# Values of latent attention for two pairs at once, store by tiles, and feature sums in two rounded parts

## The reference

```python
def rms_norm(x, w):
    xf = x.astype(jnp.float32)
    y = xf * lax.rsqrt(jnp.mean(xf * xf, axis=-1, keepdims=True) + NORM_EPS)
    return (y * w.astype(jnp.float32)).astype(x.dtype)
...
    q = (rms_norm(cq, q_lora_norm) @ w_uq).reshape(bsz, seqlen, H, MLA_NOPE + MLA_ROPE)
    kv = (rms_norm(ckv, kv_lora_norm) @ w_ukv).reshape(bsz, seqlen, H, MLA_NOPE + MLA_V)
    k_nope, v = jnp.split(kv, [MLA_NOPE], axis=-1)
...
    q_nope = rms_norm(q_nope, q_nope_norm)
    q_rope = apply_rope(rms_norm(q_rope, q_rope_norm), cos[:, None, :], sin[:, None, :])
    k_nope = rms_norm(k_nope, k_nope_norm)
...
        p = jax.nn.softmax(jnp.where(mask, s, -jnp.inf), axis=-1).astype(v.dtype)
        return jnp.einsum('bhqk,bkhv->bqhv', p, v)
```

## Time and profile before

| | us |
|---|---|
| median of 3 runs | 2898.31 |
| the profiled execution | 2898.93 |
| its span in the trace | 2897.1 |
| TensorE matmul busy | 2864.6 (99%) |
| TensorE weight load busy | 2326.3 (80%) |
| GpSimd busy | 1848.9 (64%) |
| VectorE busy | 1301.5 (45%) |
| ScalarE busy | 565.8 (20%) |

### The profile page before, as it was taken

One profiled execution on the slowest core, in us unless ns is written; L12 is line 12 of the kernel. 1 busy time (PEld: TensorE's weight loads), 2 busy tenths in 40 slices (PEclk: granted clock), 3 DMA queues, 4 the chain that ended last, 5 costly groups with the idle time before them and its releaser, 6 DMA issues.

```text
span 2897.1 us, 36332 instructions
## 1 busy us (share of the span) xinstructions
PE 2864.6 (99%) x13536; PEld 2326.3 (80%) x13536; DVE 1301.5 (45%) x1506; ACT 565.8 (20%) x821; POOL 1848.9 (64%) x1822
## 2 busy tenths in 40 slices
PE   9999999999989999999999999999999999999998
PEld 6778888888867778888888888788888777788887
DVE  5765545414355654414444223444244455543241
ACT  4550221000124541000111101210001445300000
POOL 5557548777752238777775565677777544677775
PEclk9999999999999999999999999999999999999999
DMA  4112213232220102222232222222322111222322
GB/s 152 61 60 88 74 57 111 80 108 100 84 85 28 38 29 87 92 103 102 80 125 85 74 94 81 73 100 80 105 95 91 69 63 54 72 95 84 106 92 89
DMA packets 38583, 242.35 MB, mean 84 GB/s; under 512 B 4288, under 2 KB 4672, under 8 KB 16608
## 3 DMA queue, kind: packets, MB, share of 16 engines
...
## 4 chain that ended last, share of the span: by engine, by line
PE 94%; DVE 3%; ACT 1%; DVEq 1%; issue 0%; ACTq 0%; DMA 0%; SPq 0%
PE ps L402 67%; PE ps L435 13%; PE ps L1345 1%; PE ps L1161 1%; PE ps L1301 1%; PE ps L1180 1%; PE ps L1382 1%; PE ps L1362 1%; PE ps L1395 1%; PE ps L1377 1%; PE ps L1291 1%; DVEq L2262 0%; DVEq L1857 0%; PE ps L1053 0%; DVE scr L2235 0%
## 5 line engine op out<-in xcount | busy, mean ns | idle before, releaser
L716 POOL CAST w_hi<-raw 128x512 fp32r<-128x512 f32 (+1 forms) x909 | 677.5, 761 | 1030.7 <-PE ps L402 836.7
L704 POOL TENSOR_TENSOR w_lo<-raw,w_hi 128x512 fp32r<-128x512 f32 (+1 forms) x909 | 1220.0, 1354 | 0.1
L402 PE MATMUL ps<-h_hi,w_hi 128*128 128x512 f32 x1904 | 751.7, 395 | 3.3 <-DVE h_lo L1868 3.0
L402 PE MATMUL ps<-h_hi,w_lo 128*128 128x512 f32 x1904 | 742.0, 390 | 0.0
L402 PE MATMUL ps<-h_lo,w_hi 128*128 128x512 f32 x1904 | 741.5, 389 | 0.0
L402 PEld LDWEIGHTS ps<-h_hi,w_hi 128*128 128x128 f32 x1904 | 357.8, 188 | 80.8 <-issue 5.3
L402 PEld LDWEIGHTS ps<-h_hi,w_lo 128*128 128x128 f32 x1904 | 357.6, 188 | 75.7
L402 PEld LDWEIGHTS ps<-h_lo,w_hi 128*128 128x128 f32 x1904 | 357.9, 188 | 75.1 <-issue 2.9
L402 PE MATMUL ps<-a_hi,w_hi 128*128 128x512 f32 x816 | 319.7, 392 | 2.2 <-issue 1.4
L402 PE MATMUL ps<-a_hi,w_lo 128*128 128x512 f32 x816 | 318.3, 390 | 0.0
L402 PE MATMUL ps<-a_lo,w_hi 128*128 128x512 f32 x816 | 318.1, 390 | 0.0
...
## 6 DMA issues: line engine op xcount, KB each, us to landing
...
raw<-weights SPq DMA_DIRECT2D x8, 512.0 KB, 3.5
x<-x_in SPq DMA_DIRECT2D x8, 256.0 KB, 6.3
x_out<-x SPq DMA_DIRECT2D x1, 2048.0 KB, 6.3
...
```

Source lines behind the costliest of these rows:

```text
L402: mm = pe.matmul(out_ap, a, b, start=(i == 0 and not begun), stop=(i == n - 1 and ended))
L704: pool.tensor_tensor(w_lo[:, slot, parts[j]], raw[:, slot, parts[j]], w_hi[:, slot, parts[j]].bitcast(F32), ALU.subtract).then_inc(s_split ...
L716: pool.tensor_copy(w_hi[:, slot, piece], raw[:, slot, piece]).then_inc(s_hi[j], 1)
```

## The change

Five parts:

1. The norms' sum of squares and retention's are split by VectorE into a rounded part and a remainder, and ones are copied rounded. TensorE takes two float32r matmuls where it took a float32 one.
2. In gated linear attention tile 0 of block 1 goes ahead of the last mean.
3. The values of two pairs are projected together. Chunks of even pairs hold 1536 columns (queries, keys, values of two pairs), those of odd pairs 1024. `proj_v` runs in pairs 1, 3 and 5, in two parts of 12 matmuls of 256 columns, and for pairs 0 and 1 ahead of the loop.
4. Queries are handled by heads: mean, root, scaling and rotation of head 0, then of head 1. Mean 0 goes ahead of the turned scores of head 0, keys ahead of the turned scores of head 1. At the head of the stage, VectorE's five constant copies go to ScalarE, as does the rotary part of k for the second buffer, and the two latents for keys and values come between the queries' remainders.
5. Each tile of `x` is stored as soon as it is final.

```diff
+                k, v = (i["w_ukv"][0].reshape(256, 16, 2, 64)[:, :, part].reshape(256, 1024) for part in range(2))
+                kv = [k[:, 128 * u:128 * u + 128]] + ([v[:, 128 * u:128 * u + 256]] if u % 2 == 0 else [])
+                kv = cols_of(*kv)
+                out.append(np.concatenate([q, block(kv, slice(0, 256), slice(0, kv.shape[1]))], axis=1))
...
-STAGE_WIDTHS = {"ssd": [384] + [2048] * 15, "gla": [2048] * 15, "mla": [2048] * 3 + [1280] * 8 + [2048] * 4,
+STAGE_WIDTHS = {"ssd": [384] + [2048] * 15, "gla": [2048] * 15, "mla": [2048] * 3 + [1536, 1024] * 4 + [2048] * 4,
...
         norm_sq = scr[:, scratch_len - 8 * T:scratch_len].rearrange("p (k t) -> p k t", k=8)
+
+        n_hi, n_lo, n_ones = a_hi[:, 6, :], a_lo[:, 6, :], a_hi[:, 5, 0:P]
...
-            sp.wait_ge(s_res, 8 * n_res + 2)
-            sp.dma_start(out, x[:, :, :]).then_inc(s_out, 16)
-            sp.wait_ge(s_out, 16)
+            for k in range(KD):
+                sp.wait_ge(s_res, 8 * (n_res - 1) + k + 3)
+                sp.dma_start(out[:, k, :], x[:, k, :]).then_inc(s_out, 16)
+            sp.wait_ge(s_out, 16 * KD)
...
             def norm(name):
                 pe.wait_ge(s_acc, norm_of[name])
-                pe.matmul(ps[:, norm_bank(name), :], ones, norm_sq[:, 0, :], start=True, stop=True).then_inc(s_mean, 1)
+                pe.matmul(ps[:, norm_bank(name), :], n_ones, n_hi, start=True, stop=False)
+                pe.matmul(ps[:, norm_bank(name), :], n_ones, n_lo, start=False, stop=True).then_inc(s_mean, 1)
...
+                residual_begun("gla", (0,), 1)
                 mean(hd)
-                residual_begun("gla", range(6), 1)
+                residual_begun("gla", range(1, 6), 1)
...
+
+                def proj_v(w, part):
+                    if part == 0:
+                        pe.wait_ge(s_mln, 2 * w + 2)
+                    else:
+                        pe.wait_ge(s_mr, 3 * w + 3)
+                    for tb in (2 * part, 2 * part + 1):
                         s = slice(tb * P, (tb + 1) * P)
-                        mm = product(pe, ps[:, 7, s], [(h_hi[:, k, s], h_lo[:, k, s], *kv_weights(par, k, P))
-                                                       for k in range(2)])
-                    mm.then_inc(s_used, 1)
-
-                def q_means(w):
-                    for e in range(2):
-                        pe.wait_ge(s_msl, 2 * w + e + 1)
-                        pe.matmul(ps[:, 6 + e, :], m_blkq, m_sqh[:, e, :], start=True, stop=False)
...
+                    pe.matmul(ps[:, 6 + e, :], m_blkq, m_sqh[:, e, :], start=True, stop=False)
+                    pe.matmul(ps[:, 6 + e, :], m_blkq, m_sql[:, e, :], start=False, stop=True).then_inc(s_mm, 1)
 
                 def k_mean(w):
...
 
-                    pe.wait_ge(s_mv, u + 1)
...
+                    if ahead:
+                        q_mean(u + 1, 0)
+                    else:
                         residual_begun("mla", (2,))
                     scores_turned(u, par, 0)
                     if ahead:
-                        q_means(u + 1)
+                        q_mean(u + 1, 1)
+                        proj_k(u + 1, nxt)
                     else:
                         residual_begun("mla", (3,))
                     scores_turned(u, par, 1)
                     if ahead:
-                        proj_k(u + 1, nxt)
-                        proj_v(u + 1, nxt)
+                        if par:
+                            proj_v(u + 1, 0)
                         k_mean(u + 1)
                     weighted(u, par, 0)
+                    if ahead and par:
+                        proj_v(u + 1, 1)
...
-                q_means(0)
+                pe.wait_ge(s_mcr, 3)
+                q_mean(0, 0)
+                q_mean(0, 1)
                 pe.wait_ge(s_mh, 5)
                 proj_k(0, 0)
                 k_mean(0)
                 proj_v(0, 0)
+                proj_v(0, 1)
+                pe.wait_ge(s_mkrope, 2)
                 pair(0, 0, True, True)
                 with pe.Fori(0, 3) as i:
...
                     pe.wait_ge(s_radd, hd + 1)
-                    pe.matmul(ps[:, 4, :], ones, r_sq[:, 0, :], start=True, stop=True).then_inc(s_rsum, 1)
+                    pe.matmul(ps[:, 4, :], r_ones, r_sqh, start=True, stop=False)
+                    pe.matmul(ps[:, 4, :], r_ones, r_sql, start=False, stop=True).then_inc(s_rsum, 1)
...
-                def q_squared(w, first=False):
+                act.activation(m_ident, phase_const("mla", "mla_ident"), ACT.Copy)
+                act.activation(m_mask, phase_const("mla", "mla_mask"), ACT.Copy)
+                act.activation(m_blkq, const("blkq"), ACT.Copy)
...
+                def q_rstd(w, e):
+                    act.wait_ge(s_mm, 3 * w + e + 1)
+                    act.activation(m_r[:, e, :], ps[:, 6 + e, :], ACT.Ln, bias=EPS).then_inc(s_mln, 1)
+                    settled().activation(m_r[:, e, :], m_r[:, e, :], ACT.Exp, scale=-0.5).then_inc(s_mr, 1)
...
+                def v_copied(w, n, slot, part):
+                    if slot == 0 and part:
+                        wait_used(c0 + 3 + w)
+                    elif slot == 0:
+                        act.wait_ge(s_mvp, n + 1)
+                    ins = act.activation(
+                        m_v[:, slot, 2 * part:2 * part + 2, :].rearrange("p t (x n) -> p t x n", x=3)[:, :, 0:3:2, :],
+                        ps[:, 7 - part, :].rearrange("p (t w e n) -> p t w e n", t=2, w=2, e=2)[:, :, slot, :, :], ACT.Copy)
+                    if part:
+                        ins.then_inc(s_mv, 1)
 
...
-                def pair(u, par, first, ahead):
+                def pair(u, par, ahead, n):
                     if ahead:
                         q_squared(u + 1)
+                        q_rstd(u + 1, 0)
                     exps(u, 0)
                     if ahead:
-                        q_rstd(u + 1)
+                        q_rstd(u + 1, 1)
+                        k_squared(u + 1, not par, n)
                     exps(u, 1)
                     if ahead:
-                        k_squared(u + 1)
-                        v_copied(u + 1, 1 - par, first)
                         k_rstd(u + 1)
+                    if ahead and par:
+                        v_copied(u + 1, n, 0, 0)
                     sums_inverted(u, 0)
+                    if ahead and par:
+                        v_copied(u + 1, n, 0, 1)
                     sums_inverted(u, 1)
-
+                    if ahead and par:
+                        for part in range(2):
+                            v_copied(u + 2, n, 1, part)
+
+                q_squared(0, True, (0,))
...
+                q_rstd(0, 1)
+                k_squared(0, False, 0)
                 k_rstd(0)
-                v_copied(0, 0, True)
-                pair(0, 0, True, True)
+                act.wait_ge(s_mkrope, 1)
+                act.activation(m_k[64:112, 1, :, :], m_k[64:112, 0, :, :], ACT.Copy).then_inc(s_mkrope, 1)
+                for slot in range(2):
+                    for part in range(2):
...
                 dve.wait_ge(s_sq, 8 * n + k + 1)
-                ins = settled().tensor_tensor(norm_sq[:, 0, :], norm_sq[:, 0, :], norm_sq[:, k, :], ALU.add)
+                settled().tensor_tensor(norm_sq[:, 0, :], norm_sq[:, 0, :], norm_sq[:, k, :], ALU.add)
                 if k == KD - 1:
-                    ins.then_inc(s_acc, 1)
+                    dve.tensor_copy(n_ones, ones)
...
-                    rope_in_k(w)
+                                      ALU.add).then_inc(s_mkrope, 1)
+
...
-                def q_normed(w):
+                def q_ready(w, par, e):
                     dve.drain()
-                    dve.wait_ge(s_mr, 2 * w + 1)
-                    dve.scalar_tensor_tensor(m_raw[:, 0:2, :], m_raw[:, 0:2, :], m_qgain, m_r[:, 0:2, :],
-                                             ALU.mult, ALU.mult)
+                    dve.wait_ge(s_mr, 3 * w + e + 1)
+                    dve.scalar_tensor_tensor(m_raw[:, e, :], m_raw[:, e, :], m_qgain, m_r[:, e, :], ALU.mult, ALU.mult)
                     dve.drain()
-                    turned_products(m_t, m_raw[:, 0:2, :], True)
-
-                def q_ready(par):
-                    dve.tensor_tensor(m_q[:, par, :, :], m_raw[:, 0:2, :], over_heads(cos), ALU.mult)
-                    settled().tensor_tensor(m_q[64:112, par, :, :], m_q[64:112, par, :, :], m_t[64:112, :, :], ALU.add)
+                    turned_products(m_t[:, e, :], m_raw[:, e, :])
...
-                    dve.tensor_scalar(h_hi[:, 6 + e, :], cos, 0.0, None, ALU.mult)
                 q_square_low(0, 0)
                 dve.wait_ge(s_mcr, 3)
+                latent_normed(3)
                 q_square_low(0, 1)
-                for k in (3, 4):
-                    latent_normed(k)
-                q_normed(0)
-                q_ready(0)
+                latent_normed(4)
+                q_ready(0, 0, 0)
...
```

(4 more changed lines are left out.)

87 lines of the change are left out of this document (41 added, 46 removed).

## The result

The changed kernel takes 2878.76 us, the median of 4 runs (2877.41 to 2880.24), against 2898.43 for the kernel before, run beside it: a ratio of 0.993, with a 95% interval of 0.9915 to 0.9946. It is faster by 19.7 us, 0.7%. I had forecast 2874 with a range of 2867 to 2881. The profiled execution took 2880.04 us with a span of 2878.2, 18.9 us under the span of before; my sum had said 24.2.

The account below looks back on a forecast made before the run. The prediction took TensorE as the bound, near a tie in latent attention's pairs with the chain TensorE, ScalarE, VectorE. Terms 4.4 + 1.4 + 4.4 + 10.7 + 3.3 = 24.2 us off 2898.93 gave 2874.7, median 0.6 lower: 2874; range 2867 to 2881.

Parts of the forecast that it names:

- Gain 0.40 x 11, all on the path: Norms and retention means: two products of rounded parts save 0.40 us at each of 11 sums, 4.4 us in all.
- I take no cost: Norms and retention: VectorE's three added operations, at most 3.5 us, fit in 3.7 to 3.9 us of room.
- Weights are never waited for: Whole kernel: no row of TensorE's waits names GpSimd or a DMA.
- I kept 11.2 us: Head of latent attention: the 11.2 us from the start of k's product to the first scores stay unchanged.
- the clock stays up: Rival, head of latent attention: shorter idle pieces keep the clock up; gain 28 us, 2870 us; chance 0.12.
- The forecasts of 23.6 and 25.7: Latent attention: pairs without values last 23.6 us, released by VectorE's k gains; pairs with values last 25.7.
- pairs 0, 2, 4, 6 gain 2.4 each: Latent attention: the pairs without values shrink to 23.6 us, a gain of 2.4 us each.
- pair 7 has no successor and stays: Latent attention: the last pair keeps its time, with no gain or loss.
- The full stop: Rival, shared port: VectorE loses 3.7 us per pair without values, which lasts 24.9; 2879 us; chance 0.17.
- The cold pair: Rival, latent attention: long idle time drops the clock, up to 20 us more per pair; 2966 us; chance 0.01.
- my point of 3.65: Latent attention: pairs turn cold if VectorE's chain ends over 3.65 us behind TensorE.
- The store that does not shrink: Rival, final store: the tail is a fixed cost or stores queue; gain 20.9 us, 2877 us; chance 0.12.

Follow-up runs that it names:

- second profile of the changed kernel: The changed kernel with nothing altered, run again with more runs: 2878.93 us, median of 5; its profile has a span of 2877.1 us.
- 2.9 alone: The kernel before with only the sums in two rounded parts (7 norms, 4 retention means): 2895.46 us in 10 runs, ratio 0.9987.
- 1.37 undone: The changed kernel with gated linear attention's tile 0 of block 1 put back behind the last mean: 2882.38 us, one run.
- 6.3 alone: The kernel before with only latent attention's changes, head and pairs together: 2885.96 us in 5 runs, ratio 0.9958.
- 4.25 alone: The kernel before with only the store of x by tiles: 2894.28 us in 10 runs, ratio 0.9988.
- run with casts: The changed kernel with each of GpSimd's two casts of a chunk without values made five times in pairs 0, 2 and 4: 2879.38 us, 4 runs.
- doubled run: The changed kernel with GpSimd subtracting twice for low parts of chunks without values in pairs 0, 2 and 4: 2892.77 us in 10 runs.

## Why the prediction was right, and where its steps were off

The time fell into the range, and faster was right. But parts 1 and 4 gained 6.1 us less than I had said and parts 3 and 5 2.1 us more, so the time owes its place in the range in part to errors that cancel. The terms, in us gained (measured against the second profile of the changed kernel, whose clock at the start was that of before):

| term | predicted | measured |
|---|---|---|
| 1, sums in two parts | 4.4 | 2.9 (2.9 alone) |
| 2, gated linear attention | 1.4 | 1.3 (1.37 undone) |
| 3, head of latent attention | 4.4 | 5.5 (5.3 first profile, 6.3 alone) |
| 4, pairs | 10.7 | 6.1 (7.4 first profile, 7.0 alone) |
| 5, store by tiles | 3.3 | 4.3 (4.25 alone) |
| sum | 24.2 | 20.0 |

*Part 1.* "Gain 0.40 x 11, all on the path" was right for the four means and four of the norms. "I take no cost" was wrong at the end of feed-forward stages. I had taken 3.7 us of room against at most 3.5 us of work; the work took 3.61 (1.31 + 0.68 + 1.62) and, with the gaps between, ended at 462.26, while the weight load of TensorE ahead of the norm's was over at 461.95. I had charged nothing for it, and I had not asked what VectorE's new work does to GpSimd: its last two subtractions there took 3.15 us and not 2.53, and the low weight part came 0.5 us late. "Weights are never waited for" was true of the kernel before and false of the changed one.

*Part 2* was right, down to the wait of 0.2.

*Part 3* had the mechanism and the time of k's product right: I said 4.4 us earlier; it started at 859.49 and before at 862.8, with this trace 1.4 us behind at that stage's norm, so 4.7, of which 0.4 belong to the norm of part 1. From there to the first scores I kept 11.2 us, and it took 10.3, since the clock rose during the value products, which took 3.9 us and not 5.0. That is part of the rival "the clock stays up", and it was left out of my sum. The rest of that rival did not come: with the clock back by 860 us in the second profile the stretch took 10.0 us, since VectorE's chain then held the first scores.

*Part 4* is where the sum fell short. The forecasts of 23.6 and 25.7 were measured as 23.7 to 24.1 and 25.7, VectorE releases the short pairs, and the loss to GpSimd was 2.1 us against the 2.4 that I took (without it, the chain ended at 21.6 and not at 21.2). What failed is "pairs 0, 2, 4, 6 gain 2.4 each" for pair 6, and "pair 7 has no successor and stays". The chunk that GpSimd splits in pair 6 is not one of 1024 columns: the next one in its buffer belongs to the residual and has 2048. Its four casts and four subtractions ran beside VectorE's chain from 1033.5 to 1043.9 (the last two subtractions beside k's gains, which took 3.19 us and not 1.51), so the pair took 26.06 us, gained nothing, and left TensorE idle for 3.5 us; pair 7 then lost 1.7 to 2.7 at the low clock. Releasing the chunk later gave the 9.8 us back, which is shown by experiment; that the stretching comes from the subtractions for the most part is shown by doubling them and by the run with casts. The rows of pair 6, GpSimd's subtractions and VectorE's gains of k:

```profile
1035.13 1.71 POOL L710 TENSOR_TENSOR w_lo<-raw,w_hi 128x512 fp32r<-128x512 f32 x1
...
1037.83 1.71 POOL L710 TENSOR_TENSOR w_lo<-raw,w_hi 128x512 fp32r<-128x512 f32 x1
...
1040.52 3.37 POOL L710 TENSOR_TENSOR w_lo<-raw,w_hi 128x512 fp32r<-128x512 f32 x2
```

```profile
1041.25 3.19 DVE L2283 SCALAR_TENSOR_TENSOR scr<-scr,par 64x512 f32<-64x512 f32 x2 [0.15 <-issue]
```

The 6.1 us also hold a gain that is not the pairs' own. Before, pair 0 lasted 27.4 us where the others took 26.0, as it began with the clock down:

```profile
872.00:877.00 5.00, 5.00 (x18) 4.21 (x18) 0.08 (x1) 0.60 (x1) 2.61 (x4) 0.50 0.00 0
```

The changed kernel's pair 0 ran with the clock up, and this 1.4 us I had named only under the rival of the clock. Without it the pairs gained 4.7 us of the 10.7.

*Part 5* was right in kind and 1 us too small: the slope from a 512 KB load gave 3.0 us, and the store took 2.0. The Trainium skill (DMA: Bandwidth & Descriptors, "Anatomy of one DMA — SWDGE (gpsimd) path") has its fixed 2.0 us for transfers that GpSimd issues, and this store is issued by SyncE; my estimate from it, 2.6, was nearer, and the measurement is below both.

*The rivals.* The full stop gave 2879 us, almost the measured time, but not by its mechanism: pairs without values would have lasted 24.9, and lasted 23.7 to 24.1. The rule of the Trainium skill (SBUF — State Buffer, "SBUF: two separate sides") excludes a VectorE operation with two SBUF inputs and a GpSimd operation that reads SBUF. For subtractions the runs come near to it, 0.7 to 0.8 us lost for each us of GpSimd's own work; for casts, which read SBUF as well, they do not, 0.4. The cold pair did happen, once, with an idle time of 3.5 us, and in the doubled run with 3.2; both are under my point of 3.65. But I had priced it at up to 20 us, a whole pair at 1.2 GHz, and it costs 1.4 to 2.9: TensorE is busy again at once, and the clock is back within some 4 to 7 us. The store that does not shrink fell.
